# w_attn_up's products in four PSUM banks, the first rows of the merged product turned before the last block of w_rwkv_up, and the four sums made by GpSimd

## The reference

```python
gate_attn, gate_rwkv = jnp.split(jax.nn.sigmoid(z_gate), 2, axis=-1)
merged = gate_attn * (o_attn @ w_attn_up[i]) + gate_rwkv * (o_rwkv @ w_rwkv_up[i])
h = h + rmsnorm(merged @ w_out[i], mix_post_norm[i])
```

## Time and profile before

| | us |
|---|---|
| median of 3 runs | 919.01 (918.81 to 919.24) |
| the profiled execution, its own time | 919.63 |
| its span in the profile | 917.8 |
| PE busy | 895.9 (98%) |
| DVE busy | 604.5 (66%) |
| ACT busy | 451.7 (49%) |
| POOL busy | 43.3 (5%) |

### The profile page before, as it was taken

One profiled execution on the slowest core, in us unless ns is written; L12 is line 12 of the kernel. 1 busy time (PEld: TensorE's weight loads), 2 busy tenths in 40 slices (PEclk: granted clock), 3 DMA queues, 4 the chain that ended last, 5 costly groups with the idle time before them and its releaser, 6 DMA issues.

```text
span 917.8 us, 15449 instructions
## 1 busy us (share of the span) xinstructions
PE 895.9 (98%) x6584; PEld 756.1 (82%) x6584; DVE 604.5 (66%) x961; ACT 451.7 (49%) x728; POOL 43.3 (5%) x61
## 2 busy tenths in 40 slices
PE   7999999999899999999999999999999999999997
PEld 5999888787689888888789878776778798888885
DVE  4577977556856666657665577877863456666673
ACT  4775434436534444447444357473522445555561
POOL 0010000010000000000000440000000000000000
PEclk9999999999999999999999999999999999999999
DMA  9544333124469665555429674352817566665531
GB/s 338 185 138 139 109 106 113 54 89 149 179 243 282 187 193 200 195 184 184 138 91 236 147 232 140 95 185 95 269 46 207 138 184 184 186 184 196 200 105 46
DMA packets 131204, 150.78 MB, mean 164 GB/s; under 512 B 11808, under 2 KB 102176, under 8 KB 131008
## 3 DMA queue, kind: packets, MB, share of 16 engines
q1 hardware_dynamic: 129920, 145.57, 51.1%
q10 hardware_dynamic: 1216, 4.23, 1.2%
HBM read 148.73 MB, written 1.05 MB: 163 GB/s over the span
## 4 chain that ended last, share of the span: by engine, by line
PE 86%; DVE 7%; ACT 3%; issue 2%; DMA 1%; POOL 0%; POOLq 0%; ACTq 0%; DVEq 0%
PE psum L828 11%; PE psum L718 9%; PE psum L720 8%; PE psum L719 8%; PE psum L833 7%; PE psum L781 5%; PE psum L801 4%; PE psum L802 4%; PE psum L810 4%; PE psum L724 3%; PE psum L887 2%; PE psum L877 2%; PE psum L878 2%; PE psum L834 2%; PE psum L1710 2%
## 5 line engine op out<-in xcount | busy, mean ns | idle before, releaser
L1813 ACT ACTIVATE parts<-low 128x1024 fp32r<-128x1024 f32 (+3 forms) x250 | 252.2, 1044 | 78.7 <-PE psum L720 58.0
L2689 DVE TENSOR_TENSOR parts<-low,parts 128x1024 fp32r<-128x1024 f32 (+3 forms) x154 | 185.7, 1235 | 26.8 <-ACT parts L1813 26.4
L718 PE MATMUL psum<-parts 128*128 128x512 f32 (+2 forms) x424 | 170.0, 401 | 1.8 <-DVE parts L2689 1.0
L720 PE MATMUL psum<-parts 128*128 128x512 f32 (+2 forms) x424 | 163.5, 386 | 0.0
L719 PE MATMUL psum<-parts 128*128 128x512 f32 (+2 forms) x424 | 163.4, 385 | 0.0
L1813 ACT ACTIVATE high<-psum 128x512 f32<-128x512 f32 (+4 forms) x94 | 51.8, 562 | 159.7 <-PE psum L834 74.6
L828 PE MATMUL psum<-parts 128*128 128x512 f32 x448 | 113.3, 392 | 0.0
L718 PEld LDWEIGHTS psum<-parts 128*128 128x128 f32 x424 | 79.6, 188 | 23.1 <-issue 3.8
L828 PEld LDWEIGHTS psum<-parts 128*128 128x128 f32 x448 | 84.3, 188 | 16.4
L720 PEld LDWEIGHTS psum<-parts 128*128 128x128 f32 x424 | 79.6, 188 | 16.3
L719 PEld LDWEIGHTS psum<-parts 128*128 128x128 f32 x424 | 79.8, 188 | 14.7 <-issue 0.7
(11 more groups left out here) (321 smaller groups left out, 1325.0 us busy)
## 6 DMA issues: line engine op xcount, KB each, us to landing
low<-in_w_in_dram SPq DMA_DIRECT2D x40, 1024.0 KB, 5.2
low<-in_w_ffn_in_dram SPq DMA_DIRECT2D x44, 512.0 KB, 5.2
low<-in_w_ff_in_dram SPq DMA_DIRECT2D x16, 1024.0 KB, 6.0
low<-in_w_ff_out_dram SPq DMA_DIRECT2D x16, 1024.0 KB, 4.9
low<-in_w_ffn_out_dram SPq DMA_DIRECT2D x11, 1024.0 KB, 4.9
low<-in_w_out_dram SPq DMA_DIRECT2D x8, 1024.0 KB, 5.3
low<-in_w_ple_gate_dram SPq DMA_DIRECT2D x4, 1024.0 KB, 5.0
low<-consts_dram ACTq DMA_DIRECT2D x1, 2142.0 KB, 9.1
```

The lines of the kernel that those rows point to most:

```text
L718: mm(o, l[0], r[0], start, False)
L720: return mm(o, l[1], r[0], False, stop)
L1813: return e.activation(o, a, ACT.Copy)
L2689: tt(rslot3(n, nk, width)[:, r, 0:w], slot3(n, nk, width)[:, r, 0:w], st.hi3(j)[:, r, 0:w].bitcast(F32), ALU.subtract) \
```

## The change

It does four things. The a blocks take banks 0, 2, 3, 1 in place of the cycle. DVE reads them later: all four reads are moved from the turns of `up_a` into those of `rwkv_up`. The four sums are issued by POOL (`add`) instead of DVE, under a new counter `up_pool`. The transposes of rows 0 of `mt` stand on PE before r(1,1) and no longer behind it; with them the third and fourth quarter of `w_out` are split by ACT before the high part of these rows is made, and the fourth quarter is loaded to slot 0, which a(1,1) frees, while the feed-forward's first weights take slot 2. The second rows are turned into banks 7 and 4 (before 7 and 5).

```diff
+        def turned_bank(tag, i, b):
+            return {"wo1": (5, 6, 7, 4), "pg": (5, 6, 7, 5), "wo2": (5, 6, 7, 5)}[tag][2 * i + b]
...
-            squares("wo1", (3, 5, 1, 2))
-            ring = (0, 4, 3, 5, 2, 1)
+            squares("wo1", (3, 5, 1, 0))
+            ring = (2, 4, 3, 5, 0, 1)
             q.wait_ge(*rw_dve.at("o", 1))
             e.dma_start(xr, x_d).then_inc(xr_in.land("xr"), 16)
-            q.wait_ge(*up_dve.at("m", 1, 1))
+            q.wait_ge(*up_pool.at("m", 1, 1))
...
@@ PE
-                yield from up3("r", 4, rw_bank)
+                rows = up3("r", 4, rw_bank)
+                for n in range(4):
+                    if n == 3:
+                        yield from turn_parts("wo1", 0, mt, up_pool.at("m", 0, 1))
+                    next(rows)
+                    yield
...
-            ups = up3("a", 2, pg)
+            ups = up3("a", 2, iter((0, 2, 3, 1)))
...
-            turns.alone(turn_parts("wo1", 0, mt, up_dve.at("m", 0, 1)))
...
-            turns.beside(first_rows, turn_parts("wo1", 1, mt, up_dve.at("m", 1, 1)), 1)
+            turns.beside(first_rows, turn_parts("wo1", 1, mt, up_pool.at("m", 1, 1)), 1)
...
@@ DVE
             def rwkv_up():
+                reads_a = up("a", [main_act.at("g1", 1, 1)], read_a, iter((0, 2, 3, 1)))
+                reads_r = up("r", [main_act.at("g1", 3, 1)], read_r, rw_bank)
                 up_rows("r", 1, 1)
-                for n, _ in enumerate(up("r", [main_act.at("g1", 3, 1)], read_r, rw_bank)):
+                next(reads_a)
+                for n in range(4):
+                    if n < 3:
+                        next(reads_a)
...
+                    next(reads_r)
                     split_wo("wo1", n // 2, (n % 2,))
...
                 stt(x, half_of(gates_sb, i, 2 + n), 1.0, p, ALU.add, ALU.mult).then_inc(up_dve.up("r", i, n), 1)
-                q.wait_ge(*up_dve.at("a", i, n))
-                q.wait_ge(*up_dve.at("r", i, n))
-                tt(half_of(mt, i, n), half_of(mt, i, n), x, ALU.add).then_inc(up_dve.up("m", i, n), 1)
...
@@ POOL
+            def add(i, n):
+                x = half_of(mt, i, n)
+                q.wait_ge(*up_dve.at("a", i, n))
+                q.wait_ge(*up_dve.at("r", i, n))
+                tt(x, x, tm[2 * i + n], ALU.add).then_inc(up_pool.up("m", i, n), 1)
```

More of the change, by code:

```diff
@@ L572, in program @@
         at_pe, at_act, at_dve = [count("attn_" + n) for n in ("pe", "act", "dve")]
-        up_pe, up_act, up_dve = [count("up_" + n) for n in ("pe", "act", "dve")]
+        up_pe, up_act, up_dve, up_pool = [count("up_" + n) for n in ("pe", "act", "dve", "pool")]
         wo_pe, wo_act, wo_dve = [count("wo_" + n) for n in ("pe", "act", "dve")]
@@ L654, in sync_program @@
             down("dn1", ring, 16)
-            squares("pg", (3, 5, 2, 0))
+            squares("pg", (3, 5, 0, 2))
             head("in2", w2in, (4, 1))
@@ L739, in turn_parts @@
                 for b in range(2):
-                    n = 5 + (2 * i + b) % 3
+                    n = turned_bank(tag, i, b)
                     p = bank(n)
@@ L2227, in rwkv_up @@
                         split_wo("wo1", n, *over)
+                    if n == 2:
+                        for m in (2, 3):
+                            split_wo("wo1", m, *over)
+                    if n == 3:
+                        yield from turn_parts("wo1", 0)
                     yield
@@ L2240, in scalar_program @@
             turns.alone(ups)
-            turns.alone(turn_parts("wo1", 0))
-            for n in (2, 3):
-                split_wo("wo1", n, *over)
             def block():
@@ L3107, in up_a @@
             def up_a():
-                reads = up("a", [main_act.at("g1", 1, 1)], read_a)
                 for n in range(4):
@@ L3111, in up_a @@
                         up_columns("r", 1 + n)
-                    next(reads)
                     yield
@@ L3147, in vector_program @@
             turns.alone(ups)
-            turns.alone(turn_parts("wo1", 0))
             for n in (2, 3):
                 split_wo("wo1", n)
+            for _ in turn_parts("wo1", 0):
+                pass
             def block():
@@ L3750, in rwkv @@
                 yield from normed(1)
-                yield from steps(4)
+                for n in range(4):
+                    if n == 3:
+                        yield from steps(2)
+                    add(n // 2, n % 2)
+                    yield
+            def add(i, n):
[3 more added lines that the diff above has]
+                tt(x, x, tm[2 * i + n], ALU.add).then_inc(up_pool.up("m", i, n), 1)
             def attention():
@@ L3768, in gpsimd_program @@
             turns.alone(ups)
-            turns.alone(steps(2))
             def seam(tag, i, post, more=3):
```

## The result

| | median us | runs | ratio to before |
|---|---|---|---|
| before, in the same comparison | 919.39 (918.81 to 919.73) | 7 | |
| changed | 921.52 (920.17 to 922.57) | 7 | 1.0024 [1.0014, 1.0033] |

The forecast was 919.5, in a range of 918.1 to 921.2. The measured median lies 0.3 us outside, on the slow side. That the change makes the kernel slower is clear of noise; that its time lies outside the range is not, since the interval of the ratio reaches from 920.7 to 922.4 us. Its runs also spread more than those of before, and go with their mean granted clock: 920.17 us at 0.998, 921.5 at 0.996, 922.57 at 0.995. The profile is of the slowest of them, 922.57.

What follows compares the result with a forecast made beforehand. PE, busy 98% of the span, was taken to bound the kernel, so only closing its holes pays. Terms 0.23 + 0.5 - 0.47 + 0.5 - 0.36 + 0.1 = +0.5 us gave 919.5 us, range 918.1 to 921.2.

Steps and rivals of the forecast that it cites:

- The place of the wait: PE's wait for ACT's later gate moves to a(0,0), which starts at 233.63; the hole is 3.59 us where there were 2.11.
- the rival in which both holes close: Among the a blocks: a(0,0) starts at 230.04, the late gate needed by a(1,1) only; 3.1 us faster, 915.9; chance 0.12.
- Term 1: At the a blocks: r(0,0) starts on PE at 239.21 instead of 238.98, +0.23 us.
- Terms 2 and 4: PE waits for POOL's sums at the transposes of rows 0 and of the second rows, +0.5 us each.
- Terms 3 and 5: Wait ahead of the w_out product hidden behind r(1,1), -0.47; waits inside it for last-quarter splits gone, -0.36, and +0.1.
- The starved POOL: Rival: POOL's last sum comes only behind all five DVE splits, PE stands 5.1 us; 924.1; chance 0.12 with other POOL waits.

## Why the prediction was wrong, point by point

- **The place of the wait: right.** The gate's wait moved from a(0,1) to a(0,0), which started at 233.59 for a forecast 233.63, and no other hole stood among the a blocks. This decided the sign against the rival in which both holes close; that rival's time, 915.9, is what the kernel takes once the banks are in the other order (916.52, or 915.90 with the sums on VectorE).
- **Term 1, +0.23: the step that failed.** The prediction said that all else of PE's work was the same number of the same instructions, and priced each at 0.227 us and the restart at 0.13, taken from holes of 2.1 and 1.0 us. For a hole of 3.4 that price does not hold: the term left out what the lower clock costs, and put it at nothing without a reason. Term 1 was 2.87 in the profile, 2.64 more than forecast; in the medians the clock is worth 1.3 us (the changed kernel against the one with the hole filled), since not every run loses the same. The Trainium skill has this, in TensorE: Matmul & The Clock Gate (Why this matters for your kernels): long idle gaps between bursts of matmuls bring the lower clock back. The trace agrees, 0.50 granted behind the hole. The page speaks against just this edit and was not weighed.
- **Terms 2 and 4, +0.5 each: right.** PE had issued r(1,0) at 241.85 + 36 x 0.227 = 250.02 and began the transposes at 250.52; for the second rows it was at 254.20 + 12 x 0.227 = 256.92 and began at 257.41.
- **Terms 3 and 5: right.** There is no idle time ahead of the product with w_out; from the second rows' first transposes to the third parts are 5.57 us, before 5.88: 0.31 less, forecast 0.26. The last quarter of w_out was issued at 242.04, behind a(1,1) and so as late as PE was, and ACT copied it at 247.02; both were forecast 2.6 and 2.0 us sooner, and nothing waited for it.
- **The sum without the clock** is 30.52 against 30.29 in the stretch, 0.2 more, forecast 0.5; with the hole half or wholly filled the kernel is 0.4 and 0.8 us over the one before, at the edge of what can be measured.
- **The starved POOL** did not show: the last sum took 2.19, behind one split of five.

Open stays why the clock fell inside the hole in one execution (at 232.5, 1.1 us before a(0,0)) and behind its end in two others (behind the first matmul with the sums on VectorE, behind the sixth with the banks alone), why it then slowed 14 steps in the first and 9 in the others, and whether it fell at all in the changed kernel's fastest run (920.17, mean clock 0.998); only one execution of each version has a trace.

## What to carry to other kernels

A wait goes with a bank, not with a block: before giving blocks more banks, look up what each bank's last reader is and when it is done, and give the latest one to the block that comes last. Moving a wait ahead of work that used to cover part of it makes one long hole from two short ones, and its price is not the sum of their prices: here holes of 3.1 to 3.2 us by the record also took the clock down for the matmuls behind them, in most executions and not in all. Look at the granted clock before taking the step of a matmul as a constant. A tensor operation moved to GpSimd beside VectorE instructions with two SBUF inputs took turns with them here, and cost whoever came second; TensorE waited for it, and with VectorE busy for 66% of the span there was nothing to gain on the other side.

## What was not expected of the hardware

By the idle time of the records, matmuls of one shape started 0.43 us apart for up to 12 steps behind waits of 3.19, 3.22 and 3.10 us, and 0.227 apart behind waits of 1.95 and 1.39 us in the same place and 0.84 us twelve matmuls on. In one trace the clock fell while TensorE still waited, 2.3 us after its last issue. Adding 1.9 or 3.7 us of matmuls whose results nobody reads made the kernel 1.3 to 1.7 us faster.
